# Memory queries by halves, the first query chunk by token tile, and sparse attention by pairs of heads of the two groups

## What is computed

```
h = x + concat(conv(x), nsa(x)) @ w_out            # conv and sparse attention side by side
h = h + memory_attention(rmsnorm(h), rmsnorm(mem)) # 4 heads of 256, 256 memory tokens
h = h + peer(rmsnorm(h))                           # 8 heads, 16 experts each, of 16384
out = rmsnorm(h)

# nsa: 8 heads of 64 in 2 groups; head = 4*g + jj; keys and values belong to the group g
#   out = g0 * attention over 31 compressed tokens
#       + g1 * attention over the selected blocks (here: all of them, causal)
#       + g2 * attention over a window of 512     (here: causal)
# memory_attention: q = hn @ w_q, then softmax(q k^T / 16) v, then @ w_o
# peer: q = hn @ w_q; s = q @ sub_keys; top 16 of each half, top 16 of the 256 sums
#   a = gelu(hn . u[expert]); y = sum over 128 experts of gate * a * v[expert]
```

## Time and profile before

| | |
|---|---|
| median of the runs | 2760.3 us |
| the profiled execution | 2757.09 us |
| its span, first to last instruction | 2755.1 us |
| TensorE / VectorE / ScalarE / GpSimd busy | 89% / 53% / 25% / 22% of the span |
| granted TensorE clock, mean | 0.953 |
| moved by DMA | 657.18 MB, 239 GB/s over the span |
| first gather issued | 1408.17 us |

### The profile page before, as it was taken

How to read it: one execution, slowest core, us unless ns; L and a number is a source line. 1 busy time by engine, 2 the same in 40 slices (tenths; PEclk the granted TensorE clock), 3 DMA queues, 4 the chain that set the end, 5 groups by cost and what they waited for, 6 DMA issues and landing times.

```text
span 2755.1 us, 23152 instructions
## 1 busy us (share of the span) xinstructions
PE 2448.9 (89%) x7690; PEld 1252.7 (45%) x7690; DVE 1448.1 (53%) x3802; ACT 685.3 (25%) x1633; POOL 610.8 (22%) x567
## 2 busy tenths in 40 slices
PE   6999999999999999999969898888888878788886
PEld 2456554435554455444644444444433334343332
DVE  0010331135531956431167677777777767677775
ACT  2000013116411133421224322223222222222222
POOL 0002000010000000000024443444444434344441
PEclk9999999999999979899989999999999999999999
DMA  7102241100012100012269999999999999999996
GB/s 322 61 31 99 118 194 49 61 0 1 38 61 85 71 31 31 5 57 86 83 243 404 401 416 422 421 422 422 421 422 421 421 422 420 422 421 422 421 421 271
DMA packets 83942, 657.18 MB, mean 239 GB/s; under 512 B 9410, under 2 KB 9698, under 8 KB 11378
## 3 DMA queue, kind: packets, MB, share of 16 engines
q0 software_dynamic: 75904, 552.21, 48.5%
q1 hardware_dynamic: 7922, 103.50, 9.7%
HBM read 653.58 MB, written 2.10 MB: 238 GB/s over the span
## 4 chain that ended last, share of the span: by engine, by line
PE 57%; DMA 28%; DVE 9%; issue 2%; ACT 2%; POOL 0%; DVEq 0%; POOLq 0%; PEldq 0%; ACTq 0%
DMA arena<-in_peer_uv,newton 27%; PE psum L561 22%; PE psum L1132 11%; PE psum L631 3%; DVE arena L2128 2%; PE psum L938 2%; PE psum L955 2%; PE psum L1074 1%; PE psum L611 1%; PE psum L777 1%; PE psum L1101 1%; PE psum L727 1%; PE psum L971 1%; PE psum L946 1%; PE psum L785 1%
## 5 line engine op out<-in xcount | busy, mean ns | idle before, releaser
L1132 PE MATMUL psum<-arena 128*128 128x512 f32 x2048 | 981.7, 628 | 217.9 <-ACT arena L1485 214.6
L2128 DVE CUSTOM_DVE_ANT_0 arena<-arena 128x1024 f32<-128x1024 f32 x512 | 620.9, 1224 | 284.7 <-DMA arena<-in_peer_uv,newton 279.3
L2286 POOL DMA_INDIRECT arena<-in_peer_uv,newton x512 | 568.0, 1109 | 812.1 <-PE psum L1132 704.7
L1132 PEld LDWEIGHTS psum<-arena 128*128 128x128 f32 x2048 | 398.9, 200 | 711.3 <-issue 706.4
L561 PE MATMUL psum<-arena 128*128 128x512 f32 (+3 forms) x1568 | 604.2, 546 | 11.5 <-DVE arena L1657 3.6
L561 PEld LDWEIGHTS psum<-arena 128*128 128x128 f32 (+1 forms) x1568 | 294.3, 189 | 319.1 <-issue 307.5
L1193 ACT ACTIVATE arena<-psum 128x512 f32<-128x512 f32 (+11 forms) x311 | 166.7, 545 | 723.4 <-PE psum L561 308.5
L1485 ACT ACTIVATE arena<-ident,newton 128x128 f32<-128x128 f32 x512 | 177.8, 394 | 268.4 <-DVE newton L2137 253.6
L1476 ACT ACTIVATE arena<-arena 128x2 f32<-128x2 f32 (+1 forms) x258 | 52.5, 203 | 665.2 <-DVE arena L2128 661.3
L1101 PE MATMUL psum<-arena 128*128 128x256 f32 x512 | 129.3, 379 | 0.7 <-DVE arena L1732 0.5
L1101 PEld LDWEIGHTS psum<-arena 128*128 128x128 f32 x512 | 97.0, 190 | 62.2 <-issue 54.8
(11 more groups left out here) (299 smaller groups left out, 2029.3 us busy)
## 6 DMA issues: line engine op xcount, KB each, us to landing
arena<-in_weights SPq DMA_DIRECT2D x48, 2048.0 KB, 9.0
arena<-in_peer_uv,newton POOLq DMA_INDIRECT x512, 26.5
arena<-in_xin POOLq DMA_DIRECT2D x1, 3072.0 KB, 17.6
arena<-in_dft_l POOLq DMA_DIRECT2D x1, 2048.0 KB, 15.5
arena<-in_cmp_w POOLq DMA_DIRECT2D x1, 2048.0 KB, 7.5
out<-arena SPq DMA_DIRECT2D x4, 512.0 KB, 11.8
arena<-in_pool_band POOLq DMA_DIRECT2D x1, 1280.0 KB, 5.7
arena<-in_fnet_w POOLq DMA_DIRECT2D x1, 1024.0 KB, 22.3
```

The costliest lines, as they stand in the source:

```text
L1132: ins = mm(bank(j_y[t][q]), DIAG[i % 4], ROW[ROW_PLACE[i]][:, D + 512 * q:D + 512 * q + 512], start=first, stop=last)
L2128: v.tensor_tensor_reduce(out=u, in0=u, in1=HNT[ITEM_TILE[i // 16]][:, :], scale=1.0, scalar=0.0, op0=ALU.mult, op1=ALU.add, accum_out=DOTS ...
L2286: g.indirect_dma_start(out=ROW[ROW_PLACE[i]][:, :], out_offset=None, in_=a["peer_uv"], in_offset=bass.IndirectOffsetOnAxis(ap=IDX[:, n, e: ...
```

## The change

- **Slots.** The first four blocks get four slots of their own (the fourth in memory that is not yet in use); x is loaded by the SyncE queue as the fifth transfer. The last two ring blocks (`mem_o`) go to a fifth slot at 176 KB, loaded once `out2` is done, and to the slot of the first `mem_q` block. The first load of `PQW` is issued ahead of the last ring block.
- **Sparse attention** runs over 32 pairs: the same jj, tile and branch for both groups. Scores of a pair stand behind each other (rows 0 to 63, then 64 to 127, into two banks); the value matmuls of a pair alternate between the two halves of the output. VectorE takes both maxima, then one negation; one reciprocal, then two scalings; two convolution taps per pair for 16 pairs. The compressed part is done for both heads at once (4 times instead of 8), on 31 columns instead of 128; its transposes become matmuls with the identity.
- **Memory queries** are formed per half of the tokens (64 matmuls of 256 columns for each half). The first half's 8 chunks and 4 of the second half are interleaved with the attention of the first half; the last 4 chunks of the second half run after the token transposes, ahead of `query_steps(1)`.
- **First query chunk**: head 0 is formed for token tile 0, then tile 1 (matmuls of 128 columns), and the key scores of tile 0 are computed before the second half of tile 1's queries; the token transposes move behind them.
- **Gathers**: places 4, 5 and 6 (80, 16 and 24 KB) now wait until the last `mem_q` block has been used.

```diff
-BLOCK_SLOT = [b % RING if b < FIRST_OF_TWO else (b - FIRST_OF_TWO) % 2 for b in range(N_BLOCKS)]
+BLOCK_SLOT = [b if b < 4 else (b - 1) % RING if b < FIRST_OF_TWO else (b - FIRST_OF_TWO + 1) % 2 for b in range(N_BLOCKS)]
+QUERY_SLOT = BLOCK_SLOT[N_RING - 4]
+FREE_SLOT = BLOCK_SLOT[N_RING - 3]
+BLOCK_SLOT[N_RING - 2] = 4
+BLOCK_SLOT[N_RING - 1] = QUERY_SLOT
-ROW_KB = [48, 56, 64, 72, 80, 176, 184, 40, 160, 16, 24, 32, 96, 112]
+ROW_KB = [48, 56, 64, 72, 80, 16 * FREE_SLOT, 16 * FREE_SLOT + 8, 40, 160, 176, 184, 32, 96, 112]
...
-        ITEMS2 = [(hh, qt, br) for hh in range(8) for qt in range(4) for br in range(2)]
+        ITEMS2 = [(2 * jj + g, qt, br) for jj in range(4) for qt in range(4) for br in range(2) for g in range(2)]
...
+            for b in range(N_RING):
+                if b == 4:
+                    sp.dma_start(X[:, :, :].rearrange("p a b -> p (a b)"), a["xin"]).then_inc(S["inputs_loaded"], 16)
+                if b == N_RING - 1:
+                    load_queries(0)
+                if b >= 4:
+                    sp.wait_ge(S["w_used"], max([c for c in range(b) if BLOCK_SLOT[c] == BLOCK_SLOT[b]], default=first_block["out2"] + 1) + 1)
+                load(b, BLOCK_SLOT[b])
...
+            def scores2(p):
+                for i in (2 * p, 2 * p + 1):
+                    claim(pe, j_s2[i])
+                for i in (2 * p, 2 * p + 1):
...
+                    done(mm(bank(j_s2[i], n), q, src[r:r + 64, 0:n], start=True, stop=True), j_s2[i])
+            def values2(p):
...
+                read_out(pe, j_pt2[2 * p:2 * p + 2])
                 for kt in range(qt + 1):
+                    for g in range(2):
+                        ins = mm(bank(jo, P, qt * P, p0=64 * g, p1=64 * g + 64), VSW[:, kt, P * br + 64 * g:P * br + 64 * g + 64],
+                                 PT2[:, (2 * p + g) % 4, kt * P:(kt + 1) * P], start=False, stop=(last and kt == qt))
+            for p in range(32):
+                if p < 30:
+                    scores2(p + 2)
+                if p % 8 == 2 and p < 24:
+                    cmp_scores(p // 8 + 1, 0)
+                transpose2(2 * p)
+                transpose2(2 * p + 1)
...
+                if p >= 1:
+                    values2(p - 1)
...
+                memory_step(2 * p)
+                memory_step(2 * p + 1)
...
+            for c in range(5):
+                memory_queries(0, c)
+            scores3(0, 0)
+            memory_queries(0, 5)
+            scores3(0, 1)
+            memory_queries(0, 6)
+            transpose3(0, 0)
+            memory_queries(0, 7)
+            transpose3(0, 1)
+            values3(0, 0)
+            memory_queries(1, 0)
+            scores3(0, 2)
+            memory_queries(1, 1)
+            scores3(0, 3)
+            transpose3(0, 2)
+            values3(0, 1)
+            memory_queries(1, 2)
+            transpose3(0, 3)
+            values3(0, 2)
+            memory_queries(1, 3)
             values3(0, 3)
...
+            first_queries(0, 0)
+            first_queries(0, 1)
+            first_queries(1, 0)
             pe.wait_ge(S["subk_loaded"], 16)
+            first_scores(0)
+            first_queries(1, 1)
+            token_major(j_tx[0][0], X, 0, 0)
+            first_scores(1)
+            for m in range(1, 4):
+                token_major(j_tx[0][m], X, 4 * (m % 2), m // 2)
+            for m in range(4):
+                token_major(j_th[0][m], HA, 4 * (m % 2), m // 2)
+            for c in range(4, 8):
+                memory_queries(1, c)
             query_steps(1, 0, 2 * KC)
             key_scores(1)
...
+            for p in range(32):
+                weigh2(p)
+                if p < 30:
+                    masked_max(p + 2)
+                if p % 8 == 2 and p < 24:
+                    cmp_shift(p // 8 + 1)
+                if p < 16:
+                    conv_taps(2)
...
+                    elif kb == 80 or kb < 32:
+                        pool.wait_ge(S["w_used"], N_RING - 2)
+                    elif kb in (176, 184):
                         pool.wait_ge(S["mem_o_used"], 2)
```

More of the change, by code:

```diff
@@ L342, in build @@
         bank_free = [sem(f"bank_free{b}") for b in range(8)]
-        w_full = [sem(f"w_full{s}") for s in range(RING)]
+        w_full = [sem(f"w_full{s}") for s in range(RING + 2)]
         names = """w_used small_loaded inputs_loaded const_ready dve_step cond_ready mod_ab_ready mod_cd_ready
@@ L455, in build @@
         j_o2 = [None] * 4
[L456 to L465 removed]
+        for jj in range(4):
+            j_o2[jj] = J.take(6 + jj % 2)
+            j_cs[jj] = J.take(5)
+            j_cpt[jj] = J.take(5)
+        j_ln_cv_var = J.take(5)
+        for i in range(64):
+            j_s2[i] = J.take(i % 2)
+            j_pt2[i] = J.take(3 + i % 2)
         j_mk += [J.take(2) for _ in range(4)]
@@ L473, in build @@
         j_mv += J.turn(2)
-        j_mq = J.turn(8)
+        j_mq = [[J.take(6 + c % 2) for c in range(8)]]
+        j_mq.append([J.take(6 + c % 2) for c in range(4)])
         j_s3 = [[J.take(h % 2) for h in range(4)]]
         j_pt3 = [[J.take(2 + h % 2) for h in range(4)]]
-        j_o3 = [[J.take(4 + h) for h in range(4)]]
+        j_o3 = [[J.take(4 + h % 2) for h in range(4)]]
         J.align()
@@ L514, in load @@
             def load(b, slot):
-                sp.dma_start(wring[:, slot, :, :, :].rearrange("p a k m -> p (a k m)"), a["weights"][b, :, :])\
+                sp.dma_start(slots[slot].rearrange("p a k m -> p (a k m)"), a["weights"][b, :, :])\
                   .then_inc(w_full[slot], 16)
-            for b in range(N_RING):
-                if b >= RING:
-                    sp.wait_ge(S["w_used"], max(c for c in range(b) if BLOCK_SLOT[c] == BLOCK_SLOT[b]) + 1)
-                load(b, BLOCK_SLOT[b])
             def load_queries(m):
@@ L527, in load_queries @@
                   .then_inc(S["pq_full"], 16)
-            for m in range(6):
+            for b in range(N_RING):
[6 more added lines that the diff above has]
+                load(b, BLOCK_SLOT[b])
+            for m in range(1, 6):
                 load_queries(m)
@@ L930, in scores2 @@
[L930 to L938 removed]
+                if g == 0:
+                    ins.then_inc(S["cmp_first"], 1)
+                else:
+                    done(ins, j)
@@ new lines, in cmp_transpose, with cmp_values @@
+            def cmp_transpose(jj):
+                j = j_cpt[jj]
+                claim(pe, j)
+                pe.wait_ge(S["cmp_ready"], jj + 1)
+                for qt in range(4):
+                    for g in range(2):
+                        ins = mm(bank(j, P, qt * P, p0=64 * g, p1=64 * g + N_CMP), PC[:, 4 * g + qt, 0:N_CMP], ident[:, :],
+                                 start=True, stop=True)
+                done(ins, j)
+            def cmp_values(jj):
+                jo = j_o2[jj]
+                claim(pe, jo)
+                read_out(pe, [j_cpt[jj]])
+                for g in range(2):
+                    r = 64 * g
+                    ins = mm(bank(jo, L, p0=r, p1=r + 64), VCT[r:r + N_CMP, r:r + 64], PTC[r:r + N_CMP, :],
+                             start=True, stop=False)
+                ins.then_inc(S["cmp_pt_used"], 1)
@@ L1019, in _, with memory_queries @@
                 memory_values(1, t, 0, KC)
-            pe.wait_ge(S["h_ready"], 32)
-            for b in range(2):
-                w = weights("mem_q", b)
-                for c in range(4):
-                    feat(j_mq[4 * b + c], w[:, c, :, :], H, 0, L)
-                release_block(j_mq[4 * b + 3])
-            read_out(pe, j_mk + j_mv + j_mq)
+            read_out(pe, j_mk + j_mv)
+            def memory_queries(s, c):
+                w = weights("mem_q", c // 4)
+                j = j_mq[s][c]
+                claim(pe, j)
+                for k in range(KC):
+                    if c == 0:
+                        pe.wait_ge(S["h_ready"], 24 + 8 * s + k + 1)
+                    ins = mm(bank(j, HL), w[:, c % 4, k, :], HM[:, s, k, :], start=(k == 0), stop=(k == KC - 1))
+                done(ins, j)
+                if s == 1 and c % 4 == 3:
+                    release_block(j)
             def scores3(s, h):
@@ L1991, in _ @@
                 add_chunk(SUM2[:, :], SQ[:, c, 0:L], c == 0)
-            invert(j_rms_mq[0], RS2[:, :], D)
-            rms_apply(RS2[:, :], "memq_g", X, H, L)
+            invert(j_rms_mq[0], RSM2[:, :], D)
+            for s in range(2):
+                for k in range(KC):
+                    v.scalar_tensor_tensor(out=HM[:, s, k, :], in0=X[:, k, HL * s:HL * s + HL], scalar=vc("memq_g", k),
+                                           in1=RSM2[:, HL * s:HL * s + HL], op0=ALU.mult, op1=ALU.mult).then_inc(S["h_ready"], 1)
+            counts["h"] += 2 * KC
             def row_max3(s, h):
```

413 lines of the change are left out of this document (207 added, 206 removed).

## The result

The changed kernel takes 2676.3 us (median of four runs, 2673.3 to 2678.6) against 2759.5 for the kernel before in the same runs: a ratio of 0.970, 95% interval 0.9683 to 0.9717. That is 83 us less. The direction was right, a size was wrong. The profiled execution took 2673.3 us, with a span of 2671.4.

What follows compares the result with a forecast made beforehand. Bound: TensorE ahead of the first gather, then the gathers' DMA. Profiled 2757.1 - 1 (start) - 41 (sparse stage) - 19.6 (memory queries) + 5.5 (first queries, gathers) = 2701; median 3.2 higher, 2704 us, range 2688 to 2732.

Steps and rivals of the forecast that it cites:

- (7n + 1) u + 0.63 = 2.61 us: Sparse stage: TensorE time per pair of n tiles (mean 2.5), u = 0.107 us per 128-column instruction, 0.63 for group changes.
- 3n u: Sparse stage: a pair's score time, u per 128-column instruction, n tiles; partial overlap, between 2n u (full) and 4n u (none).
- "+1" of the values: Sparse stage: a pair's alternating value matmuls cost (2n + 1) u instead of 4n u, one instruction over full overlap.
- My count of the last stretch: Check of the unit costs on the old sparse stage's last stretch: items, memory steps, compressed parts make 54 us, against 53.3.
- rival B: Sparse stage: a pair's scores overlap fully, 2n u instead of 3n u; 8.6 us less, 2695 us; chance 0.12.
- I give 3 us back: Sparse stage, pairs with convolution taps: VectorE stays under TensorE's time with little left; 3 us lost.
- I give back 8: Sparse stage, convolution's norm: cover gone while silu and table loads hold ScalarE and scalings hold VectorE; 8 us lost.
- "3" at the ends of the stage: Sparse stage: a pair waits for both members, maxima at the start and copies at the end; 3 us lost.
- rival A: Sparse stage: the round trip sets the pair loop, not TensorE; stage saves only 20 us, 2725 us; chance 0.18.
- D: Sparse stage stays at the lower clock, only column halves overlapping: 254 us, +36, total 2781 us, slower; chance 0.04.
- The gathers' start: Start of gathers: second query-weight load falls into the saturated stage, +5 us, and DMA runs dry before the tenth gather, +3.
- Rival C: Gathers: second query load lands late, at 26.5 us, and the ring runs dry 14.5 us more; 2719 us; chance 0.08.

Runs made afterwards that it cites:

- the two halves: Against the kernel before: only the sparse attention changed, 2696.5 us, ratio 0.9772; only all the rest of the change, 2742.8 us, ratio 0.9947.

## Why the prediction was wrong

The miss lies in the sparse stage. This is where its time went, TensorE's from each group's start to the next one's, added up from the timelines of the two profiles, against the terms of my sum (us):

| | before | after | less | forecast |
|---|---|---|---|---|
| pairs: scores, transposes, values | 137.7 | 81.6 | 56.1 | 48 |
| compressed part | 26.1 | 21.0 | 5.1 | 7 |
| memory keys and values | 34.9 | 30.7 | 4.2 | 0 |
| sums of the norm | 8.8 | 7.2 | 1.6 | 0 |
| waits of TensorE | 10.9 | 16.7 | -5.8 | -14 |
| stage | 218.3 | 157.1 | 61.2 | 41 |

Two steps failed, with 8 us each, and a third, with 6, was missing. None of them alone leads out of the range; together they do.

- **The first step that failed: the price of a pair, "(7n + 1) u + 0.63 = 2.61 us", and in it the "3n u" of the scores.** Adding up the starts of groups in the changed kernel at full clock, a pair of n = 2 takes 0.64 (scores, 1024.97 to 1025.61), 0.58 (four transposes) and 0.60 (eight values, 0.66 to their end): 1.82, where the formula gives 2.23; for n = 1, 3 and 4 it is 1.15, 2.36 and 3.10. The mean is 2.11, so 0.50 less than my price. Not all of that is miss, since the price of the two items before, 3.94, was too high as well. Timeline of TensorE in the kernel before:

```profile
1031.45 0.65 PE L955 MATMUL psum<-arena 128*64 128x128 f32 x4
1032.03 1.16 PE L909 MATMUL psum<-arena 64*128 64x128 f32 x8
...
1039.92 0.70 PE L938 MATMUL psum<-arena 64*128 64x256 f32 x2
1040.55 0.66 PE L946 MATMUL psum<-ident,arena 128*128 128x128 f32 x4
...
1051.95 0.44 PE L946 MATMUL psum<-ident,arena 128*128 128x128 f32 x2
1052.31 0.43 PE L955 MATMUL psum<-arena 128*64 128x128 f32 x2
...
1072.30 1.12 PE L971 MATMUL psum<-arena 128*128 128x512 f32 x2
```

  An item of n = 2 takes 0.63 (scores), 0.36 (transposes) and 0.58 (values), two of them 3.14 and not 3.40; for n = 1, 3 and 4 two take 2.07, 4.24 and 5.30, and the mean is 3.69. So a pair saves 1.58 us at full clock and not 1.33, and 0.25 for each of 32 pairs is 8 us. The scores, at 2n u instead of 3n u, are 0.27 of it, as holding them apart showed. The "+1" of the values adds 0.11, and the one set of gaps that falls away is some 0.12 smaller than my 0.63, because I had read the gap behind the scores at an unusually long place (1043.00, 0.72 to the next group, where 1039.92 has 0.63). My count of the last stretch could have told: its 54 us are to be held against the 48.89 that TensorE is busy in that stretch, not against its length of 53.3. I had the full overlap as rival B with 0.12 and 8.6 us; that mechanism came, at about that size, and doesn't give the time by itself. The Trainium skill ("TensorE: Matmul & The Clock Gate", Part 3: Packing small matmuls) gives a pack the time of one matmul and some ns a tile; the trace agrees, 0.70 us for four score instructions as for two. I had weighed that rule against a row of another form and read out of the row a limit that it doesn't show.
- **The second: the waits, "I give 3 us back", "I give back 8" and "3" at the ends of the stage.** Of 14 us 5.8 came. Timeline of TensorE, changed kernel:

```profile
1074.39 0.73 PE L967 MATMUL psum<-ident,arena 128*128 128x128 f32 x4 [1.81 <-DVE arena L2063]
...
1118.22 1.09 PE L967 MATMUL psum<-ident,arena 128*128 128x128 f32 x4 [4.20 <-DVE arena L2063]
```

  The wait at the silu is the largest, 4.20 us. The one at the norm is 1.81, no longer than the 3.06 that stood there before. VectorE did not become the bound: its row maxima still wait 34.1 us for scores (97.8 before), and it is busy 104.45 of the stage's 157.11 us, so rival A, a bound on the round trip with VectorE over 80%, did not come. Nor did D, the stage at the lower clock: 0.86.
- **The third: the work beside the pairs, which the sum held constant.** It took 6 us less. These are groups of the stage, before and then after (by line: busy us, mean ns; busy times of neighbours overlap a little, so they add up to more than the table):

```profile
L831 PE MATMUL psum<-arena 128*128 128x256 f32 x64 | 18.8, 419 | 0.0
L971 PE MATMUL psum<-arena 128*128 128x512 f32 x32 | 18.0, 645 | 0.0
L909 PE MATMUL psum<-arena 64*128 64x128 f32 x64 | 11.8, 339 | 0.0
L927 PE MATMUL psum<-arena 31*64 31x512 f32 x16 | 10.2, 725 | 0.9 <-PE psum L955 0.9
L611 PE MATMUL psum<-arena,ones 128*128 128x512 f32 x16 | 8.9, 710 | 0.0
```
```profile
L995 PE MATMUL psum<-arena 128*128 128x512 f32 x32 | 15.7, 613 | 0.7 <-ACT arena L1267 0.5 <-PE psum L977 0.2
L843 PE MATMUL psum<-arena 128*128 128x256 f32 x64 | 15.9, 392 | 0.3 <-PE psum L977 0.3
L923 PE MATMUL psum<-arena 64*128 64x31 f32 x64 | 12.0, 339 | 0.1
L623 PE MATMUL psum<-arena,ones 128*128 128x512 f32 x16 | 7.4, 605 | 0.0
L946 PE MATMUL psum<-arena 31*64 31x512 f32 x16 | 5.2, 729 | 0.0
```

  The 96 instructions of memory keys and values went from 36.8 us to 31.6. Little of that is the clock: before, all 16 groups of L971 ran at full clock (1.12 to 1.13 us each, as at 1072.30), and of those of L831 all but one. But two memory steps now stand one behind the other, so 32 groups became 16, and with each pair of steps one change of group of 0.20 us fell away (1.92 to the next group instead of 2 x 1.06). The clock gave some 0.7 us there and 1.5 in the sums of the norm, one of whose two groups took 5.24 us before and 3.70 now. The granted clock of the whole stage is nearly the same, 0.85 and 0.86.
- **The compressed part: 7 us forecast, 5.1 measured.** The 31 columns brought 1 to 2 us, not 4, and in sum the score instructions take as long as before (11.8 and 12.0 us busy). At full clock a group of eight takes 0.97 where it took 1.16 before the change and 1.05 with 128 columns after it; the row that I had priced it by the earlier trace rows has another form, with 64 columns of weights and not 128. The values brought 5.0 (10.2 to 5.2 in the rows above), not 1.7: they overlap fully as well, though ordered by half.
- **Start of the program: 1 us forecast.** Block 4 came as worked out (37.55 against 38.3) and the projection began 4.4 us earlier. I had charged the idle time before it too much. How much of the 5.5 at the start of the sparse stage is the change is less sure: that start lies anywhere from 976.2 to 982.9 in the twelve profiles with the new program start, and at 981.9 and 987.0 in the two with the old one. Within one program it moves with the clock granted from 790 to 836 us, 0.96 in one profile of the changed kernel and 0.89 in the other.
- **Memory queries: 19.6 forecast, 20.4 measured** (86.4 - 66.0), with no wait for weights. Right.
- **First queries: 2.5 forecast, 2.0 measured** (88.4 - 86.4). Right.
- **The gathers' start: 8 forecast, 4.7 given back** (88.4 - 83.7). The second query load was late as described (1335.27), the hole in the DMA is where I put it, from 1344 to 1356 at 0.87, and smaller: 1.6 us, not 3. The load itself costs less than its 5.0 us: from the first gather on the changed kernel moves 554.90 MB and the kernel before 553.49, and 1.41 MB take 3.4 us at 413 GB/s, which I read as the load issued at 1403.09 being partly still to come there too. Rival C did not come.
- **Sum.** In the two profiles 4.5 us of the miss lie at the start, 20 in the sparse stage, 3.3 at the gathers. By the times of the two halves nearly all of it is in the stage: 63 us where I had 41, and 17 where I had 15; together they make 80 of 83. So the 4.5 at the start may be the spread between executions.

Not settled: what the 31 columns are worth to a microsecond, and why the clock from 790 to 836 us differs between executions. The compared rows come from one profile of each kernel; in the second one of the changed kernel the stage is 154.8 us, with TensorE busy 2.2 us less.

## What to carry to other kernels

Before an overlap of small matmuls is priced, ask which row shows that very form, and if none does, keep full overlap as a case with real weight: the nearest row bounds only its own form. Price the kernel before with the same formula and hold the sum against TensorE's busy time, not against the length of the stretch: only the difference of the two prices counts. Ask which untouched work will stand in longer groups than before. Price a stage of small matmuls at the clock that it has and at the one that it may get: over these kernels it went from 0.79 to 0.93. To test an overlap, take it away with a wait and leave the rest, but read the single group (0.70 against 1.45 us) and not the total alone: the wait has a price of its own, and may move the clock.

## What the runs showed of the hardware

Two matmuls of 64 rows each in the two row halves, one behind the other and into two banks, run in the time of one: 0.70 us for four instructions of 256 columns, as for two, and 1.45 when one matmul waits for the other. In column halves, eight instructions ordered by half cost as much as alternating ones (0.66), sixteen cost 1.58 against 1.09. A matmul of 31 columns behind a weight of 64 rows and 128 columns costs nearly what one of 128 does (0.97 against 1.05 us for eight instructions). A change of group costs 0.15 to 0.20 us at full clock: eight instructions of 128x256 in one group take 1.92 to the next group, in two groups 2 x 1.06. The clock of TensorE in the sparse stage, 0.93 to 0.79 over these kernels, went by how the work lay: 0.79 and 0.80 where the scores were held apart, 0.88 where only the values were, 0.86 to 0.88 in the changed kernel, 0.92 and 0.93 with the dense products early. Why the scores' wait lowered it and the values' did not is open.
